# Another table of held-back work for the attention planner of a one-core decoder layer

## The reference, cut to what matters

```
proj = rms_norm(x) @ w_in
o_sb  = stick_breaking(q, k, v)                 # 4 heads, all earlier keys
o_swa = banded_attention(.., window 128, sinks) # 8 heads
o_nsa = g0*compressed + g1*selected + g2*window # 4 heads, three branches
x = x + rms_norm(concat(rms_norm(o_nsa), rms_norm(o_swa), rms_norm(o_sb)) @ w_out)
x = x + rms_norm((silu(h @ w_gate) * (h @ w_up)) @ w_down),  h = rms_norm(x)
```

## Time and profile before

| what | us |
| --- | --- |
| median of 3 runs | 1231.21 |
| lowest of them | 1225.16 |
| the profiled execution | 1226.87 |
| its span on the core | 1225.1 |
| second stage, 117 to 504 us | about 387 |

### The profile page before, as it was taken

One profiled execution on the slowest core, in us unless ns is written; L12 is line 12 of the kernel. 1 busy time (PEld: TensorE's weight loads), 2 busy tenths in 40 slices (PEclk: granted clock), 3 DMA queues, 4 the chain that ended last, 5 costly groups with the idle time before them and its releaser, 6 DMA issues.

```text
span 1225.1 us, 18755 instructions
## 1 busy us (share of the span) xinstructions
PE 1206.5 (98%) x6588; PEld 1038.9 (85%) x6588; DVE 860.0 (70%) x1638; ACT 608.9 (50%) x1172; POOL 180.3 (15%) x153
## 2 busy tenths in 40 slices
PE   9999999999999999999999999999999999999997
PEld 7899788888999999888888888888888888888886
DVE  6423697968779765446966766656657568897888
ACT  5432687757777665434743333333333345544343
POOL 5230211111000000111001112201122021000014
PEclk9999999999999999999999999999999999999999
DMA  7303411136843100223213323133231456643443
GB/s 246 122 2 122 115 42 52 35 112 163 183 109 97 26 19 18 92 98 113 94 44 112 127 88 116 65 122 129 87 125 60 143 198 223 241 154 122 151 176 138
DMA packets 66833, 137.13 MB, mean 112 GB/s; under 512 B 8551, under 2 KB 27247, under 8 KB 66740
## 3 DMA queue, kind: packets, MB, share of 16 engines
q1 hardware_dynamic: 66740, 135.93, 35.2%
HBM read 90.52 MB, written 28.60 MB: 97 GB/s over the span
## 4 chain that ended last, share of the span: by engine, by line
PE 81%; DVE 8%; issue 4%; ACT 3%; DMA 2%; SPq 1%; POOL 0%; DVEq 0%; POOLq 0%; ACTq 0%
PE ps L2544 32%; PE ps L2574 14%; PE ps L1134 8%; PE ps L2488 4%; PE ps L1114 4%; PE ps L997 4%; PE ps L978 4%; PE ps L923 3%; PE ps L1079 2%; PE ps L1087 2%; PE ps L1012 1%; DMA m_qs<-m_qn 1%; DVE ring L1511 1%; PE ps L1145 1%; DMA f_scr<-act_pairs 1%
## 5 line engine op out<-in xcount | busy, mean ns | idle before, releaser
L2544 PE MATMUL ps<-f_topH,f_W 128*128 128x512 f32 x704 | 220.7, 389 | 0.8 <-DVE f_W L2335 0.8
L2544 PEld LDWEIGHTS ps<-f_topH,f_W 128*128 128x128 f32 x704 | 132.2, 188 | 28.6 <-DVE f_W L2335 1.3
L2335 DVE TENSOR_TENSOR f_W<-f_scr,f_W 128x512 fp32r<-128x512 f32 (+1 forms) x128 | 89.6, 703 | 87.2 <-ACT f_W L2098 87.0
L2544 PE MATMUL ps<-f_topL,f_W 128*128 128x512 f32 x352 | 136.9, 389 | 0.0
L1134 PE MATMUL ps<-V,m_tw 128*128 128x66 f32 (+1 forms) x1056 | 127.8, 272 | 0.2
L2574 PE MATMUL ps<-f_headH,f_W 128*128 128x512 f32 x408 | 127.4, 389 | 0.6 <-DVE QT L2368 0.6
L1134 PEld LDWEIGHTS ps<-V,m_tw 128*128 128x128 f32 x1056 | 125.2, 192 | 2.6 <-DVE m_mix_n L1561 1.3
L2544 PE MATMUL ps<-f_headH,f_W 128*128 128x512 f32 x352 | 114.7, 390 | 0.0
L2098 ACT CAST f_W<-f_scr 128x512 fp32r<-128x512 f32 (+1 forms) x128 | 77.6, 610 | 30.1 <-PE ps L2574 14.8
L2574 PEld LDWEIGHTS ps<-f_headH,f_W 128*128 128x128 f32 x408 | 76.6, 188 | 16.9 <-issue 1.0
L2335 DVE TENSOR_TENSOR f_W<-ring,f_W 128x512 fp32r<-128x512 f32 x60 | 59.6, 1005 | 33.4 <-ACT f_W L2098 33.3
(11 more groups left out here) (283 smaller groups left out, 2647.0 us busy)
## 6 DMA issues: line engine op xcount, KB each, us to landing
act_pairs<-QT SPq DMA_DIRECT2D x77, 256.0 KB, 4.3
m_qs<-m_qn SPq DMA_DIRECT2D x128, 128.0 KB, 2.4
ring<-in_ffn_w_up SPq DMA_DIRECT2D x22, 512.0 KB, 3.7
f_stage<-act_pairs SPq DMA_DIRECT2D x40, 256.0 KB, 3.5
ring<-in_ffn_w_gate SPq DMA_DIRECT2D x19, 512.0 KB, 4.6
f_scr<-act_pairs SPq DMA_DIRECT2D x37, 256.0 KB, 3.5
ring<-in_ffn_w_down SPq DMA_DIRECT2D x11, 512.0 KB, 5.5
f_pair_up<-in_ffn_w_down SPq DMA_DIRECT2D x11, 512.0 KB, 6.9
```

Of the source, the lines that this page charges most:

```text
L2335: dve.tensor_tensor(slot_part(s, 1), source(s), slot_part(s, 0).bitcast(F32), ALU.subtract).then_inc(lo_done, 1)
L2544: ins = pe.matmul(ps[:, bank, :], whole[:, w, cols], halves[h][:, k0 + k, col:col + HALF], start=(begins and k == 0 and w == 0 and h == 0) ...
```

## The change

`HELD` gets other contents and `MOVED` becomes empty. Nothing else is touched: neither the costs in `plan_attention`, nor its rule of choice, nor any function that emits instructions. The new table was found by a search in another model of the chip, in which work of DVE that runs beside work of GpSimd takes longer by half; that model isn't in the kernel. The old table has 41 entries that sum to 53.0 us, the new one 44 that sum to 75.5 us. Seven keys stand in both, one of them with the same value.

```diff
 HELD = {
-    "combine": {36: 1000},
-    "cut_hi": {14: 1500, 16: 1500, 20: 500, 22: 2500},
-    "cut_lo": {15: 2500},
-    "half_hi": {11: 1500},
-    "half_keep": {16: 500},
-    "keep": {18: 500, 82: 500, 96: 500},
-    "logits": {78: 500, 88: 2500, 91: 500, 107: 500, 117: 1000, 179: 1000, 181: 2500},
-    "mean_squares": {21: 2500},
-    "scores": {48: 1000, 122: 1000, 134: 1000, 139: 2500, 141: 1000, 144: 1000, 170: 2500, 180: 2500, 183: 1000, 185: 1500},
-    "softmax": {157: 500},
-    "stick_combine": {2: 1000},
-    "stick_exp": {9: 2500, 18: 1500},
-    "stick_scan": {10: 500},
-    "stick_sub": {0: 500, 8: 1000, 18: 500},
-    "stick_weights": {19: 1000, 28: 2500},
-    "weigh": {12: 1000, 126: 1500},
+    "combine": {36: 500},
+    "cut_hi": {14: 1000, 16: 2500, 20: 1500, 22: 1000},
+    "cut_lo": {15: 1500},
+    "half_scale": {12: 2500, 15: 2500},
+    "keep": {17: 1000, 138: 2500},
+    "logits": {84: 1000, 97: 1500, 134: 500, 158: 1000, 175: 2500, 193: 1500},
+    "out_hi": {0: 2500},
+    "root": {1: 500},
+    "scores": {92: 2500, 93: 1500, 115: 2500, 134: 1000, 159: 2500, 167: 2500, 168: 1000, 174: 1500, 181: 2500, 204: 2500},
+    "softmax": {76: 2500},
+    "spread": {13: 500},
+    "squares": {4: 2500},
+    "stick_scan": {9: 1500, 17: 2500},
+    "stick_sub": {25: 2500, 30: 1000},
+    "stick_weights": {9: 1000},
+    "turn": {80: 2500, 93: 1500, 138: 2500},
+    "weigh": {0: 2500, 8: 1500, 24: 1000, 26: 1000, 27: 1500},
 }
 MOVED = {
-    "combine": {19: 60},
-    "logits": {93: 220},
-    "scores": {15: 400, 212: 180},
 }
```

## The result

The changed kernel takes 1234.68 us, the median of 8 runs (1233.71 to 1237.17). The kernel before, run beside it, takes 1226.72 us. The ratio is 1.0073 with a 95% interval from 1.0062 to 1.0085: 8 us more, where 2 us less than the recorded median was forecast. The profiled executions, 1234.28 against 1226.87 us, carry the same difference, so the traces can be read for it.

A forecast was written before the change was run, and what follows sets the result against it. PE was taken as the bound, busy 98% of the span. From the profiled 1226.9 us, -0.8 for collisions, +1.4 for holds and +1.5 for where a median falls gave 1229 us, range 1219 to 1243 us.

The forecast's parts named there:

- The stage as the place: The edit reaches only the planner-ordered stage from 122.4 to 503.94 us, 381.5 us long, whose end moves within 8 us.
- The third stage: Unplanned work from the first L2488 product at 503.94 us on; expected to stay 721 us long, cost nothing.
- The ceiling of 16 us: In the planned stage PE needs 365.6 of 381.5 us, so a table has some 16 us to win.
- Holds on PE's work: In the planned stage, 18 held PE pieces instead of 12, at 0.23 us each: +1.4 us, bounds -2.8 to +9 us.
- the holds on DVE and ACT: In the planned stage, 12 on DVE and 10 on ACT, costed at nothing because both idle; bound about 2.8 us either way.
- The early stall and its spell: At 136.28 us PE waits 1.74 us for queries, then the clock drops, costing 1.7 us; both expected to stay.
- Collisions: DVE work delayed beside GpSimd's L899 in the stage: eight, 6.2 us of DVE, 1.5 us reaching PE; forecast -0.8 us.
- Rival 3: The change doesn't do what it says: collisions stay as many, 1228 to 1231 us; 0.78 together with the forecast.
- Rival 2: Held `scores` and `turn` behind 348 us make PE wait for `logits`: up to 1246 us; 0.11 within 2%, 0.03 beyond.
- Rival 1: A real gain: the new order closes half or more of 12.5 us of PE waiting, 1215 to 1221 us; chance 0.07.

The follow-up runs named there:

- e7: The kernel before with one entry, `stick_sub` 18 (500 ns), taken out of its old table; ratio 1.0130, +15.9 us.
- e11: The new table, read by the kernel's planner changed so that DVE work overlapping GpSimd work takes longer by half of the overlap; ratio 1.0000.
- e12: The kernel before with its old tables, read by a planner that lengthens DVE work by half its overlap with GpSimd work; ratio 1.0066.
- e6: The changed kernel with the second stage's sixteen `half_scale` cut from 512 columns to 8, order unchanged; 1232.17 us, ratio 1.0051.
- e1: The kernel before with the new table's entries for work begun in the stage's first 130 us, old entries for the rest; 1237.67 us, ratio 1.0111.
- e5: The kernel before with the second stage's sixteen `half_scale` cut from 512 columns to 8, order unchanged; 1223.45 us, ratio 0.9969.
- e4: The kernel before with `HELD` and `MOVED` both empty; ratio 1.0148, +16.5 us.
- e2: The kernel before with old entries for work begun in the stage's first 130 us and the new table's entries for the rest; ratio 1.0060, +6.6 us.
- e3: The kernel before with its old `HELD` kept and `MOVED` (four ages) emptied; ratio 1.0026, +2.8 us.
- e8: The kernel before with one entry of the new table added, `weigh` 8 (1500 ns); ratio 1.0130, +15.2 us.
- e9: The kernel before with tables searched anew from the old ones to minimise a replay with measured durations (813 and 1052 entries); 1224.10 us, ratio 0.9993.
- e10: The kernel before with tables searched anew from empty ones to minimise a replay with measured durations (793 and 1054 entries); 1223.87 us, ratio 0.9990.

## Why the prediction was wrong

The direction was wrong: 2 us less than the recorded median was forecast, within a range of 1219 to 1243 us, and it became 8 us more than the kernel before. The range and "within 2%" held, the range because it was wide: the sum inside it had no term of the right size.

- **The stage as the place: right.** The third stage is 720.35 us long, 721 were forecast. But the first L2488 product was to be within 8 us of 503.94 us; it comes 8.2 us later, 2.25 of them from before the stage.
- **The ceiling of 16 us: not contradicted, and not tested either.** The best order tried won 5.7 us in a profile, and the gaps counted above would allow 26 us. A ceiling says nothing about what can be lost, and an edit of a tuned order has more room on that side: the plan without a table is 12 us longer.
- **"Holds on PE's work": the step that failed.** I took (18 - 12) x 0.23 = +1.4 us, a local price of one wait for each entry, and zero for the holds on DVE and ACT. Even the local price was read from the wrong engine: the 12 waits of 2.8 us are PEld's; PE itself waited for `logits` once, 0.4 us. e7 shows the price of one 0.5 us hold on one DVE subtraction, the worst of all: 15.9 us. An entry doesn't delay its work by its own amount. It changes the choice at one point, and every later choice of the list scheduler follows from that. The term was about +8.8 us in the profile, where I had a sum of +0.6 us for collisions and holds. My upper bound of +9 us came from 18 longest waits, a mechanism that isn't at work here. What would have told it is the length of the two orders, 374.1 against 381.8 us (with the holds 382.3 us), which follows from the costs in `plan_attention`.
- **The assumption behind it: wrong.** I took both tables for equals that were each searched against something like this planner. The change's own words said that the new one was found under another model, and the diff touches no cost. I read this as a question of which collisions are dodged, and not of which planner reads the entries. e11 and e12 show that it is the latter.
- **The early stall and its spell: wrong, in the kernel's favour.** I expected them to stay, as they lie ahead of nearly all held work. The stall shrank from 1.74 to 0.57 us and the spell is gone, which hid 2.9 us of the loss. Whether the table did this isn't shown. e6, whose order is that of the kernel after, waits 1.25 us at this place, and e1 with the new early entries 1.62 us; e5, with the old order, waits 0.88 us. The spell isn't in any of the three, nor in e4 behind a wait of 1.68 us; e2, e3 and e8 have it behind 1.72 to 1.76 us, and e12 behind 1.66 us. Both may differ from one execution to the next.
- **Collisions: wrong sign, small size.** I forecast -0.8 us and fewer of them. They didn't get fewer: eleven instead of eight, 8.4 us of DVE time instead of 6.2 us. The scan of 640 columns no longer collides, others do instead (the timeline below). Rival 3's mechanism is thus true, but it isn't the cause of the loss: e5 and e6 put the whole matter at 2.5 to 3.8 us in either order.
- **Rival 2: right place, other waiter.** PE does lose its time behind the last filler, 4.1 us between 348 and 400 us. But it waits little more for `logits` than before (PEld 3.6 us instead of 2.8 us); it waits for `combine`, 3.1 us that were not there. And that is 3.1 of the 8.3 us added; the others are waited for earlier, for `half_keep` and `stick_sub`. No spell at the lower clock follows in this kernel. And e1 shows that new entries behind 348 us aren't needed for it. I gave this side of zero 0.14 and priced it at 17.5 us; it was half of that.
- **Rival 1, a real gain:** nothing of it came, and e11 (1.0000) says that it wouldn't have come with the planner with the penalty either.

The collisions of the kernel after, with the scans that run alone beside them:

```profile
139.44 0.69 DVE L1510 TENSOR_TENSOR_SCAN ring<-ring 128x256 f32<-128x256 f32 x1
...
140.44 1.29 POOL L898 TENSOR_TENSOR QT<-QT 128x512 f32<-128x512 f32 x1 [6.93 <-ACT QT L1214]
140.47 1.80 DVE L1510 TENSOR_TENSOR_SCAN ring<-ring 128x256 f32<-128x256 f32 x1
...
173.51 1.22 DVE L1510 TENSOR_TENSOR_SCAN ring<-ring 128x512 f32<-128x512 f32 x1
...
175.83 1.84 DVE L1510 TENSOR_TENSOR_SCAN ring<-ring 128x512 f32<-128x512 f32 x1
...
211.02 1.27 POOL L898 TENSOR_TENSOR QT<-QT 128x512 f32<-128x512 f32 x1 [11.95 <-ACT QT L1214]
211.60 2.30 DVE L1510 TENSOR_TENSOR_SCAN ring<-ring 128x768 f32<-128x768 f32 x1
```

**What stays open.** How much e9 and e10 really win. Why the first stage has its spell at 54 us in some executions and not in others, and what brings on the spells in the stage. And what makes e2, e7 and e8 worse than their plans beyond the waits named: the medians of one class differ by up to 8 us, and only profiles of single executions stand behind the last three columns of the table.

## What to carry to other kernels

A table of exceptions for a greedy scheduler is no set of local corrections; here it was good only together with the model that it was searched in, and a table without its planner lost half of what the search had won (8.0 of 16.5 us). Price such an edit by running the planner with both tables and comparing the lengths of the two orders, not by adding up entries; and play them through without the holds, since a plan that contains them can look some 50 us longer than its order is (e9). Before a search is aimed at a contention, take the contending instruction away in one run: here that puts the whole prize at 2.5 to 3.8 us.

## What the runs showed of the hardware

**A collision costs what is left of the GpSimd instruction.** The scan of 256 columns takes 0.69 us alone. The one at 140.47 us begins 0.03 us after GpSimd's product, which has 1.26 us to go, and takes 1.80 us: 1.26 + 0.69 = 1.95 us, less 0.15. The scan of 512 columns at 175.83 us takes 1.84 us instead of 1.22; that of 768 at 211.60 us meets 0.69 us of GpSimd work and takes 2.30 us. In all 19 such collisions of the two traces, eight before and eleven after, the excess is what is left of GpSimd's product less 0.13 to 0.20 us. So the penalty is neither "half again" nor a share of the scan's length. The Trainium skill (SBUF — State Buffer, Who interferes with whom) says that the pair of ports which DVE and GpSimd share is an exclusive lock, and that a DVE instruction with two SBUF inputs needs it against a GpSimd instruction that reads SBUF; by that rule the second one waits until the first is done. The traces agree within 0.20 us. A model of the delay would be that remainder, for two-input work alone.

**The length of one wait of PE didn't tell whether the clock fell.** The wait of 1.74 us in the kernel before has a spell of 3.4 us at 1.2 GHz behind it. But in e4 a `piece` waits 2.62 us for `half_keep` and no spell follows: the granted clock stays 1.00 from 200 to 216 us. And in e12 a spell of 10.2 us begins at 400.2 us although no wait of PE in the 8 us before is longer than 0.57 us.

```profile
208.73 0.47 PE L978 MATMUL ps<-m_hH,m_wH 128*128 128x512 f32 x1 [2.62 <-ACT QT L1196]
206.00:210.00 4.00, 1.38 (x7) 1.09 (x7) 3.96 (x4) 2.55 (x5) 1.34 (x1) 1.00 0.55 133
210.00:216.00 6.00, 6.00 (x30) 5.02 (x28) 5.49 (x6) 4.06 (x7) 0.47 (x1) 1.00 0.00 0
```

```profile
392.00:400.00 8.00, 7.43 (x68) 7.19 (x66) 7.25 (x29) 5.66 (x13) 0.54 (x1) 1.00 0.43 139
400.00:404.00 4.00, 4.00 (x20) 4.00 (x19) 1.83 (x8) 1.04 (x3) 0.00 (x0) 0.52 0.27 65
```

A spell at 1.2 instead of 2.4 GHz loses at most half its length, some 5 us for the longest ones of 10.2 us (an estimate from the two levels), and less where PE waits in it anyway, as in e7.
